# Two-layer encoder trunk: the last four experts' rows stay in SBUF and are added by TensorE, the other rows are read back inside the expert loop, and GpSimd subtracts the low halves of the first GDN panel

## The reference

```
h = rmsnorm(x)
x = x + mixer(h)                      # attention in layer 0, GDN in layer 1
h = rmsnorm(x)
group  = top 1 of 4;  experts = top 2 of the 8 in that group
gate_k = g_prob * e_prob_k / sum(e_prob)
x = x + sum over the token's 2 experts of gate_k * (silu(h Wg_e) * (h Wu_e)) Wd_e
```

## Time and profile before

| | us |
|---|---|
| median of 3 runs (lowest to highest) | 1280.09 (1280.09 to 1281.01) |
| the profiled execution's own time | 1278.82 |
| its span | 1277.1 |
| PE busy | 1145.1 (90%) |
| DVE busy | 519.5 (41%) |
| ACT busy | 383.5 (30%) |
| POOL busy | 385.5 (30%) |

### The profile page before, as it was taken

How to read it: one execution, slowest core, us unless ns; L and a number is a source line. 1 busy time by engine, 2 the same in 40 slices (tenths; PEclk the granted TensorE clock), 3 DMA queues, 4 the chain that set the end, 5 groups by cost and what they waited for, 6 DMA issues and landing times.

```text
span 1277.1 us, 21577 instructions
## 1 busy us (share of the span) xinstructions
PE 1145.1 (90%) x8755; PEld 805.1 (63%) x8755; DVE 519.5 (41%) x1188; ACT 383.5 (30%) x854; POOL 385.5 (30%) x428
## 2 busy tenths in 40 slices
PE   5999999899999884989889999889999899999782
PEld 4876678655555442868568887678888555555441
DVE  4466663411111114564684455753653411111114
ACT  3426841111111102354553445543422111111010
POOL 1233621112232211047545266542301022322110
PEclk9999999999999997989999999999999899999896
DMA  7121047999999998111000120002366999999996
GB/s 241 67 73 67 2 192 277 368 364 381 383 386 379 383 392 320 69 66 67 2 3 1 67 101 31 3 2 81 151 247 261 359 372 389 388 386 377 380 390 247
DMA packets 67795, 278.24 MB, mean 218 GB/s; under 512 B 16888, under 2 KB 16984, under 8 KB 43120
## 3 DMA queue, kind: packets, MB, share of 16 engines
q1 hardware_dynamic: 56480, 255.89, 52.7%
q0 software_dynamic: 11072, 20.43, 4.7%
q10 hardware_dynamic: 144, 0.52, 0.1%
HBM read 265.83 MB, written 27.26 MB: 230 GB/s over the span
## 4 chain that ended last, share of the span: by engine, by line
PE 69%; DMA 13%; DVE 8%; ACT 4%; SPq 3%; issue 2%; POOL 1%; DVEq 0%; POOLq 0%
PE bank L1132 14%; PE bank L150 9%; PE bank L152 8%; PE bank L151 8%; DMA hn<-in_moe_w_up 8%; PE bank L1141 6%; PE bank L1676 4%; PE bank L1124 3%; DMA x<-in_moe_w_up 3%; SPq L2382 2%; PE bank L541 2%; PE bank L550 1%; PE bank L575 1%; PE bank L389 1%; PE bank L298 1%
## 5 line engine op out<-in xcount | busy, mean ns | idle before, releaser
L1002 POOL DMA_INDIRECT y_rows<-arena,idx_i x64 | 64.5, 1008 | 350.0 <-DVE arena L1319 345.0
L1224 ACT ACTIVATE arena<-bank 128x128 f32<-128x128 f32 x64 | 17.7, 277 | 368.2 <-PE bank L1132 368.2
L1323 DVE TENSOR_TENSOR arena<-arena,bank 128x128 f32<-128x128 f32 x64 | 18.4, 287 | 259.2 <-ACT arena L1224 259.2
L152 PE MATMUL bank<-ring_r,ht_r 128*128 128x512 f32 x288 | 113.0, 392 | 0.0
L1132 PE MATMUL bank<-ring,arena 128*64 128x256 f32 x832 | 101.6, 396 | 7.7 <-DMA ring<-in_moe_w_up 6.7
L1319 DVE COPY arena<-bank 128x512 f32<-128x512 f32 x64 | 44.2, 691 | 144.2 <-PE bank L1141 144.2
L150 PE MATMUL bank<-ring_r,arena_r 128*128 128x512 f32 (+1 forms) x228 | 91.3, 401 | 6.1 <-DVE ring_r L174 5.4
L151 PE MATMUL bank<-ring_r,arena_r 128*128 128x512 f32 x224 | 87.8, 392 | 0.0
L1132 PEld LDWEIGHTS bank<-ring,arena 128*64 128x64 f32 x832 | 57.9, 136 | 42.7 <-DMA ring<-in_moe_w_up 7.7
L151 PE MATMUL bank<-ht_r,ring_r 128*128 128x512 f32 (+1 forms) x224 | 80.9, 361 | 0.0
L1124 PEld LDWEIGHTS bank<-ident,arena 64*128 64x128 f32 x512 | 61.3, 201 | 28.3 <-issue 25.1
(11 more groups left out here) (343 smaller groups left out, 2338.4 us busy)
## 6 DMA issues: line engine op xcount, KB each, us to landing
ring<-in_moe_w_gate SPq DMA_DIRECT2D x26, 1024.0 KB, 21.5
ring<-in_moe_w_up SPq DMA_DIRECT2D x26, 1024.0 KB, 25.3
arena<-in_moe_w_down SPq DMA_DIRECT2D x24, 1024.0 KB, 27.5
ring<-in_moe_w_down SPq DMA_DIRECT2D x24, 1024.0 KB, 26.9
ring<-in_gdn_w_in SPq DMA_DIRECT2D x8, 2048.0 KB, 8.0
arena<-in_moe_w_gate SPq DMA_DIRECT2D x10, 1024.0 KB, 19.4
arena<-in_moe_w_up SPq DMA_DIRECT2D x10, 1024.0 KB, 23.3
ht<-in_moe_w_gate SPq DMA_DIRECT2D x10, 1024.0 KB, 27.0
```

What stands on the lines that cost most here:

```text
L152: return pe.matmul(dst, a[1], b[0], start=False, stop=stop)
L1002: pool.indirect_dma_start(out=y_rows[l], out_offset=bass.IndirectOffsetOnAxis(ap=idx_i[:, 1, e:e + 1], axis=0), in_=y_out[:, e % RING, :], ...
```

## The change

- `SENT` is 28. Only experts 0 to 27 are scattered. For experts 28 to 31, DVE multiplies each row of the down projection by its gate (`keep_y`) into `kept_y`, an area of the ring; two experts share a tile of 128 rows (a pair q holds two experts, and the tile is kept for either half ab of the columns). ACT and DVE split it in high and low parts (`kept_high`, `kept_low`).
- TensorE adds these rows to their tokens as matmuls with 0/1 matrices (`add_kept`, 32 matmuls of 128x512). The matrices are made in the loop: DVE marks slots after expert 26 (`mark_slots`), TensorE turns them after body 27 (`turn_marks`), ACT copies them at expert 28.
- `read_back` stands right behind the read of x in `moe_sync`, for both layers, into places of down weights. It is therefore issued before panel GB, and needs only the scatters up to expert 27. `fill_rows` writes x to all of `y_rows` once, in the attention stage (16 transfers of 512 KB), so that rows nobody scatters hold finite numbers; their gates are zero.
- The adds are spread: t = 0 is added by DVE inside the loop, at experts 30 and 31 (`combine_rows`), t = 1 by DVE behind the loop. For t = 2 and 3 ACT scales the rows (`scale_rows`) and GpSimd adds them to x. Then DVE adds the eight PSUM banks of the kept rows (`add_kept_dve`), t = 2 and 3 after GpSimd's adds.
- Gates are computed before the first expert instead of beside it, and TensorE sums gates to slots (8 small matmuls).
- Panel GB's low halves go to GpSimd, behind the roots of t = 0 and 1. Panel GB+1 is loaded once all adds to x are done, before it was once the last down projection was done.

The core of the diff:

```diff
+KEPT = 4
+SENT = EXPERTS - KEPT
...
-        LOW_BY = {n: "pool" if n in (3, 4) or GB < n < GB + 7 else "dve" for n in PANELS}
+        LOW_BY = {n: "pool" if n in (3, 4) or GB <= n < GB + 7 else "dve" for n in PANELS}
...
-            for e in range(EXPERTS):
+            for e in range(SENT):
                 if e + AHEAD < EXPERTS:
                     gather(e + AHEAD)
                 scatter(e)
+            pool.wait_ge(x_again, Y_FILLED + 16 * TT * (l + 1))
+            for t in (2, 3):
+                for k in range(2):
+                    pool.wait_ge(s["exp_g"], 6 + 2 * (t - 2) + k + l * PER["exp_g"])
+                    last = pool.tensor_tensor(x[:, t, :], x[:, t, :], y_in[t][:, k, :], ALU.add)
+                    if k == 0 or t == 2:
+                        o.step(last)
+            last.then_inc(s["idx"], 1)
...
+            def kept_pair(q, n):
+                t, ab = n // 2, n % 2
+                for high in (True, False):
+                    if n < 2:
+                        if high:
+                            pe.wait_ge(s["exp_e"], 2 + 2 * q + ab + l * PER["exp_e"])
+                        else:
+                            pe.wait_ge(s["dve"], 3 + 2 * q + ab + l * PER["dve"])
+                    last = pe.matmul(bank[(4 + n) % 8][:, :], spread_of(q, ab)[:, t * P:(t + 1) * P],
+                                     kept_y(q, ab, high), start=q == 0 and high, stop=q == 1 and not high)
+                return last
...
+            def scale_rows(t):
+                act.wait_ge(y_back[t], 16 + 32 * (l + 1))
+                for k in range(2):
+                    act.activation(y_in[t][:, k, :], y_in[t][:, k, :], ACT.Copy, scale=stat[:, 10 + k, t:t + 1]
+                                   ).then_inc(s["exp_g"], 1)
...
+            scale_rows(2)
+            kept_high(1)
+            scale_rows(3)
...
+                if e == SENT + 2:
+                    kept_low(0)
+                    combine_rows(dve, l, 0, 0, o)
+                if e == SENT + 3:
+                    combine_rows(dve, l, 0, 1, o)
+            keep_y(EXPERTS - 1)
+            kept_low(1)
...
+            combine_rows(dve, l, 1, 0, o)
+            combine_rows(dve, l, 1, 1, o)
+            for t in range(TT):
+                add_kept_dve(dve, l, t)
+
+        def combine_rows(dve, l, t, k, o):
+            if k == 0:
+                dve.wait_ge(x_again, Y_FILLED + 16 * TT * (l + 1))
+                dve.wait_ge(y_back[t], 16 + 32 * (l + 1))
...
+        def add_kept_dve(dve, l, t):
+            if t == 2:
+                dve.wait_ge(s["idx"], 2 + l * PER["idx"])
+            for half in range(2):
+                n = 2 * t + half
+                c = slice(half * HALF, (half + 1) * HALF)
+                dve.wait_ge(s["lists"], 2 + n + l * PER["lists"])
+                dve.tensor_tensor(x[:, t, c], bank[(4 + n) % 8][:, :], x[:, t, c], ALU.add
+                                  ).then_inc(s["combined"], 1)
...
         def read_back(sp, l):
             for i in range(RING):
                 sp.wait_ge(y_stored[i], 16 * slot_uses(l + 1, i))
+            sp.wait_ge(s["ranks"], PER["ranks"] * (l + 1))
+            sp.wait_ge(s["y_sum"], SENT + 1 + l * PER["y_sum"])
...
                 sp.dma_start(x[:, t, :], x_rows[l][t * P:(t + 1) * P, :]).then_inc(x_again, 16)
+            read_back(sp, l)
...
+            fill_rows(sp)
             moe_first(sp, 0)
...
-            used = [(s["up"], 27), (s["y_sum"], 32)] + [(g["proj"], 4), (g["proj"], 8), (g["av"], 8), (g["proj"], 16)]
+            used = [(s["up"], 27), (s["combined"], 2 * TT)] + [(g["proj"], 4), (g["proj"], 8), (g["av"], 8), (g["proj"], 16)]
...
-                if i == 0:
-                    read_back(sp, 0)
...
-            for t in range(TT):
+            for t in range(2):
+                norm_root(pool, 2, t)
+            split_low(pool, GB)
+            for t in range(2, TT):
                 norm_root(pool, 2, t)
...
-            split_low(dve, GB)
-            for t in range(2):
-                combine_best(dve, t, o)
-                combine_second(dve, t)
```

More of the change, by code:

```diff
@@ L894, in build @@
         y_out = ml.take(RING, HALF)
-        y_in = [cut(2 * D * t, 2, D) for t in range(TT)]
+        y_in = [dn_home[1 + t].rearrange("p (k n) -> p k n", k=2) for t in range(TT)]
+        y_late = [gu_home[4 + t // 2][:, t % 2 * 2 * D:(t % 2 + 1) * 2 * D].rearrange("p (k n) -> p k n", k=2)
+                  for t in range(TT)]
         ml.at = 2 * D * TT
@@ L942, in slot_uses @@
         def slot_uses(l, s):
-            return sum(1 for e in range(EXPERTS) if e % RING == s) * l
+            return sum(1 for e in range(SENT) if e % RING == s) * l
         def rows_in(l, e):
@@ L1140, in down_rows @@
                     for half in range(2):
-                        last = pe.matmul(bank[3][half * SLOTS:(half + 1) * SLOTS, :],
+                        side = half ^ turned_halves
+                        last = pe.matmul(bank[3][side * SLOTS:(side + 1) * SLOTS, :],
                                          hidden_t[:, i, m * SLOTS:(m + 1) * SLOTS],
@@ L1198, in moe_pe @@
             pick_rows()
+            gates_to_slots()
             turn(0)
@@ new lines, in moe_dve @@
+            late_passes(dve, l, None, late, late_rows)
+            combine_rows(dve, l, 1, 0, o)
+            combine_rows(dve, l, 1, 1, o)
+            for t in range(TT):
+                add_kept_dve(dve, l, t)
+        def combine_rows(dve, l, t, k, o):
+            if k == 0:
+                dve.wait_ge(x_again, Y_FILLED + 16 * TT * (l + 1))
+                dve.wait_ge(y_back[t], 16 + 32 * (l + 1))
+            o.step(dve.scalar_tensor_tensor(out=x[:, t, :], in0=y_in[t][:, k, :], scalar=stat[:, 10 + k, t:t + 1],
+                                            in1=x[:, t, :], op0=ALU.mult, op1=ALU.add))
@@ L1381, in send_out, with fill_rows @@
-                for i, c in enumerate(halves):
-                    sp.wait_ge(s["combined"], TT + t + 1 + i)
+                halves = ((slice(0, D), 2),) if t < TT - 1 else ((slice(0, HALF), 1), (slice(HALF, D), 2))
+                for c, n in halves:
+                    sp.wait_ge(s["combined"], 2 * TT + 2 * t + n)
                     sp.dma_start(out[0, t * P:(t + 1) * P, c], x[:, t, c]).then_inc(const_in, 16)
             sp.wait_ge(const_in, GDN_CONSTS_IN + 16 * (TT + 1))
+        def fill_rows(sp):
+            for l in range(2):
+                whole = y_rows[l].rearrange("(r h) n -> r (h n)", h=2)
+                for n in range(2 * TT):
+                    sp.dma_start(whole[n * P:(n + 1) * P, :], x[:, n % TT, :]).then_inc(x_again, 16)
```

203 lines of the change are left out of this document (145 added, 58 removed).

## The result

| | before | changed |
|---|---|---|
| median of 4 runs each, same chip (lowest to highest), us | 1280.55 (1280.09 to 1281.83) | 1300.11 (1298.56 to 1300.58) |
| span of the profiled execution, us | 1277.1 | 1298.9 |

The changed kernel takes 1.0149 times as long (95% interval 1.0131 to 1.0167), 19.6 us more; 1300 had been forecast. The two profiled spans differ by 21.9 (1298.93 less 1277.06), since the profiled execution of before was 1.7 under its median and that of the changed kernel 0.5 above.

What follows compares the result with a forecast made beforehand. Weights set the expert loop's pace at 383 GB/s; the change concerned the stretches behind both loops. 12.4 + 7.4 + 0.5 = 20.3 on 1278.8 makes 1299.1, median 1300.4, stated as 1300; 8-in-10 range 1283 to 1306.

Steps and rivals of the forecast that it cites:

- When y lands: SP's queue behind both loops: transfers land in issue order, y in pairs 2.9 us apart, the panel 9 us later.
- The 2.5 us credited to the missing scatters: Landing of x's last part behind each loop: 2.5 us earlier without four scatters, bounds 0 and 3.75.
- From T to the last add: Adds behind each loop, after y of t = 2 lands: 19.7 us with DVE and GpSimd alternating, 13.2 without blocking.
- The seam: Layer 0, from the expert loop to the GDN: first GDN unit done at 533.4 against 521.0, 12.4 us late.
- The tail: End of layer 1: last add at 1280.1, plus 4.4 to the span's end, 7.4 us late.
- The expert's wait inside the loop: Expert 31 runs about 6.5 us later behind the first add of y; that alone costs nothing.
- Everything else: Small gate matmuls ahead of the first transposes put expert 0 back 0.2 to 0.3 in each layer: 0.5 us.
- Rival 1: Behind both loops DVE and GpSimd run side by side without blocking: 1286.7 us, chance 0.23.
- rival 2: Behind both loops y lands 6.5 us earlier, DVE is not blocked, the kernel is faster: 1274 us, chance 0.13.
- Rival 3: Its claim is not in the text given, beyond a half clock in the first GDN unit; chance 0.08.
- Rival 4: A wash: blocking half as often and y 3 us earlier, within 0.2% of before; chance 0.06.

Runs made afterwards that it cites:

- e1: Changed kernel with GpSimd's four adds and ACT's scaling taken out, DVE adding all of t = 1 to 3: 1298.21 us, ratio 1.0158 to before.
- e4a: Changed kernel with the two adds of t = 0 moved out of the loop, behind the last `keep_y`: 1299.62 us, ratio 1.0181 to before.
- e4b: Changed kernel, t = 0 adds behind the loop and `kept_low(1)`, ACT's `kept_high(1)` ahead of the first scaling: 1290.86 us, ratio 1.0101 to before.
- e6: Kernel before with only panel GB's low halves moved to GpSimd, behind the roots of t = 0 and 1: 1284.05 us, ratio 1.003.
- e2: Changed kernel with panel GB issued ahead of y in layer 0: 1306.02 us, ratio 1.0207 to before.
- e5: Changed kernel without GpSimd adds, PSUM sums before y; layer 0: panel GB first, DVE split, t = 2, 3 adds behind first norms: 1284.44 us, ratio 1.0031 to before.
- e3: Changed kernel with panel GB's low halves back on DVE, behind the last add and ahead of the first norm: 1301.49 us, ratio 1.0186 to before.

## Why the prediction was right

Times of the changed kernel are given here in the frame of before, less 1.92 us in layer 0 and 15.32 in layer 1, by which the last expert's gate and up matmuls came later.

- **When y lands.** Forecast for t = 0: 493.0, measured 495.1 (497.00 - 1.92). For t = 2: 498.8 against 500.1, in layer 1 1260.4 against 1261.2. The panel: 507.5 against 507.6. The order is right, but two sizes are wrong and nearly cancel. The 2.5 us credited to the missing scatters did not come: x's last part landed at 492.4 (issued at 469.86, 24.5 us, less 1.92), where it had been 492.6 before and 490.1 was forecast, and in layer 1 at 1253.7 against 1254.2 before. And the 6 MB behind it, y and the panel, took 15.2 us instead of 17.4, by an estimate from these numbers 414 GB/s where I had set 383 as the limit. The close landing of the panel is luck.
- **From T to the last add.** T is the moment at which y of t = 2 has landed and ACT starts to scale it. Forecast 19.7 with alternation, 13.2 without; measured 18.8 in layer 0 (501.99 to 520.75) and 19.0 in layer 1. The rule, one instruction of DVE after each one of GpSimd, carries the prediction, and e1 shows it by taking GpSimd away: two adds of y go from 6.71 to 2.60. The Trainium skill (SBUF — State Buffer, Who interferes with whom) gave the exclusion, and the runs agree (one norm pass 3.36 beside GpSimd, 1.28 alone). That the two take turns was my addition, and the single lengths bear it out. GpSimd's third add ends at 511.47 and DVE's add behind it at 512.55, the fourth ends at 514.76 and DVE's next at 515.84. One of DVE's four passes does not wait in either layer: the first low part in layer 0 (0.68), the last add of y in layer 1 (1.28).
- **The seam.** First norm's L287 519.1 (forecast 518.9), end of the second norm 525.3 (525.5), first GDN matmul 529.4 (529.5). PE waits for the last of GpSimd's quarters alone, 0.48 us, and the last of the first unit's 24 matmuls starts at 532.9 (533.4). The seam grew by 11.9 against 12.4 forecast.
- **The tail.** 6.5 against 7.4. The last add ends at 1280.2 (forecast 1280.1), since T came 0.8 later and the way from there took 0.7 less; what was too large is the 4.4 from there to the end, now 3.4. Why the last output lands faster was not looked into.
- **The expert's wait inside the loop** costs nothing by itself, as forecast (e4a). But I had not seen that its removal is worth 8.6 together with an early high copy (e4b), because the low passes then run before GpSimd starts.
- **Everything else.** Forecast 0.5, in the profile 3.4. The sums of gates stand alone on PE for 1.84 us, and from the picking of rows to expert 0 it is 10.5 us instead of 9.7: 0.8 in each layer against 0.2 to 0.3 forecast:

```profile
251.84 1.84 PE L1231 MATMUL bank<-arena 128*128 128x4 f32 x16
```

Another 1.3 came from slower transposes near 226 us at a lower granted clock, in this execution and not in the others. From the first 96x96 matmul of the GDN to the picking of rows in layer 1 it is 474.1 against 473.2, while the second run of the same kernel shows 476.4: that scatter is not explained.
- **`fill_rows`** costs nothing: its 16 transfers are issued from 105.71 on, and SP's next issue is at 175.63, where before it was at 175.54.

The seam's 11.9 and the tail's 6.5 leave 3.4 of the 21.9 between the spans; this rest is a difference and not a measurement of its own. Against the forecast's 20.3 the profiles show 1.6 more and the medians 0.7 less. So the mechanism and its size in each seam are borne out to within 1 us, and the agreement of 1300 with 1300.11 is closer than the terms are.

Rival 1 (no blocking) is refuted by e1 and by the single lengths. Of rival 2 (y lands early) the opposite happened: y came 0.8 to 2.1 us later than forecast. Rival 3's half clock did not come in the first unit of the changed kernel, which ran at a granted clock of 1.00 from 531.3; in e6 it did. Rival 4 (a wash) needed half the blocking and is out by 19.6 us.

## What to carry to other kernels

Work given to GpSimd beside DVE passes with both inputs in SBUF was not done in parallel here: count up to one GpSimd instruction of wait for each such DVE instruction, and put beside it DVE work that reads PSUM. A transfer issued 24 us earlier in a full queue landed 9 us earlier: it gains only what the bytes ahead of it leave, and what it overtakes comes later (the panel by 9 us behind 4 MB of y, y by 5.2 behind the panel's 2 MB in e2). Before an engine is relieved of a step, look whether it was idle there: DVE's split of the panel filled a wait of 10 us, and taking it away cost 3.8 us (1.5 to 6.0). Data that lands earlier gives nothing while other work stands ahead of it on the engine that uses it (e5).

## What the runs showed of the hardware

- DVE and GpSimd take turns instruction by instruction when both read SBUF with two inputs: DVE's 128x1024 pass takes 3.36 to 3.38 us beside GpSimd (changed kernel, e6) and 1.28 alone (e3), its 128x512 pass 2.73 and 0.68, and 64-wide ones took 1.41 and 2.42 in the earlier trace rows. GpSimd suffers less: its 128x1024 pass takes 2.39 in the earlier trace rows, and in the changed kernel 2.74, 2.90 and 3.21 where a DVE pass had to end first (two in 6.03 at 508.73).
- DVE's adds with one input in PSUM are not held back: in e4b four take 2.48 at 505.05, while GpSimd adds, and 2.48 at 512.11, when it is done.
- Eight float32 matmuls with four columns each show as sixteen passes and took 1.84 us in all: that few columns do not make them free.
- In e6 the first unit's 24 matmuls of 256 columns started within 5.0 us at a granted clock of 0.50, behind an idle time of PE of 3.40 us; in the kernel before within 2.8 at 1.00, behind 1.30.
